# RWKV's token shift taken from TensorE's difference products to row transfers inside SBUF, mixed on VectorE before the gated unit

## The reference

```python
def rwkv7_mixer(z, mu, w0, w2, a0, a2, g2, k_k, k_a, r_k, ln_w, ln_b):
    z_prev = jnp.pad(z, ((0, 0), (1, 0), (0, 0)))[:, :-1]
    z = z + (z_prev - z) * mu.astype(f32)
    cuts = np.cumsum([D_RWKV, D_RWKV, D_RWKV, DECAY_LORA, ICL_LORA]).tolist()
    r, k, v, xw, xa, xg = jnp.split(z, cuts, axis=-1)
    w_log = -jax.nn.softplus(-(w0 + jnp.tanh(xw) @ w2)) - 0.5
    a = jax.nn.sigmoid(a0 + xa @ a2)
    g = jax.nn.sigmoid(xg) @ g2
    ...
```

## Time and profile before

| what | value |
|---|---|
| median of 3 runs | 1326.61 us (1326.31 to 1327.68) |
| profiled execution, span from first to last instruction | 1326.5 us (no other time is given for it) |
| TensorE busy | 1143.2 us, 86% |
| VectorE busy | 418.9 us, 32% |
| ScalarE busy | 208.0 us, 16% |
| GpSimd busy | 123.2 us, 9% |
| HBM read | 375.13 MB, 284 GB/s over the span |
| mean granted TensorE clock | 0.955 of full speed |

### The profile page before, as it was taken

One profiled execution on the slowest core, in us unless ns is written; L12 is line 12 of the kernel. 1 busy time (PEld: TensorE's weight loads), 2 busy tenths in 40 slices (PEclk: granted clock), 3 DMA queues, 4 the chain that ended last, 5 costly groups with the idle time before them and its releaser, 6 DMA issues.

```text
span 1326.5 us, 18979 instructions
## 1 busy us (share of the span) xinstructions
PE 1143.2 (86%) x8244; PEld 622.7 (47%) x8244; DVE 418.9 (32%) x820; ACT 208.0 (16%) x396; POOL 123.2 (9%) x148
## 2 busy tenths in 40 slices
PE   7989997986566676755899999999999799999996
PEld 6645454432222222222455467888776453333332
DVE  4255933110001000100148636641583531111113
ACT  3211431010000000000000114011240241211111
POOL 0010000100005880000025400000000000000000
PEclk9999998998889888889999999999999899999998
DMA  8422948999999999999923453111316639999991
GB/s 315 154 100 93 376 198 340 428 428 426 427 428 427 427 426 427 428 427 428 379 98 122 143 212 127 66 66 65 127 64 231 281 130 406 423 421 422 422 420 50
DMA packets 62397, 377.33 MB, mean 284 GB/s; under 512 B 6128, under 2 KB 7536, under 8 KB 37104
## 3 DMA queue, kind: packets, MB, share of 16 engines
q1 hardware_dynamic: 60736, 369.64, 68.4%
q10 hardware_dynamic: 1584, 6.55, 1.4%
HBM read 375.13 MB, written 1.05 MB: 284 GB/s over the span
## 4 chain that ended last, share of the span: by engine, by line
PE 62%; DMA 30%; DVE 4%; ACT 2%; issue 1%; SPq 0%; DVEq 0%; ACTq 0%
DMA arena<-in_w_expert_up 21%; PE psum L472 11%; PE psum L475 9%; PE psum L2749 7%; DMA arena<-in_expert_w_up 4%; PE psum L2773 3%; PE psum L1353 3%; PE psum L815 3%; DMA arena<-in_w_expert_gate 3%; PE psum L2784 3%; PE psum L2233 2%; PE psum L1383 2%; PE psum L2336 2%; PE psum L1062 2%; DMA arena<-in_w_expert_down 2%; PE psum L1969 1%
## 5 line engine op out<-in xcount | busy, mean ns | idle before, releaser
L1353 PE MATMUL psum<-arena 128*32 128x256 f32 x2048 | 147.0, 436 | 97.5 <-DMA arena<-in_w_expert_up 58.8
L472 PE MATMUL psum<-arena 128*128 128x512 f32 x352 | 157.6, 598 | 3.2 <-ACT arena L509 1.6
L1353 PEld LDWEIGHTS psum<-arena 128*32 128x32 f32 x2048 | 69.9, 121 | 175.8 <-DMA arena<-in_w_expert_up 74.6
L1383 PE MATMUL psum<-arena 128*32 128x512 f32 x512 | 124.2, 635 | 18.0 <-DMA arena<-in_w_expert_down 12.7
L475 PE MATMUL psum<-arena 128*128 128x256 f32 x544 | 122.9, 382 | 1.0 <-ACT arena L1790 1.0
L2749 PE MATMUL psum<-arena 128*64 128x512 f32 x512 | 116.0, 595 | 2.4 <-DMA arena<-in_expert_w_up 2.2
L475 PEld LDWEIGHTS psum<-arena 128*128 128x128 f32 x544 | 101.5, 189 | 16.9 <-issue 2.2
L472 PEld LDWEIGHTS psum<-arena 128*128 128x128 f32 x352 | 64.8, 190 | 81.4 <-issue 81.1
L1383 PEld LDWEIGHTS psum<-arena 128*32 128x32 f32 x512 | 31.3, 115 | 98.5 <-issue 69.3
L1414 DVE TENSOR_TENSOR arena<-arena,psum 128x256 f32<-128x256 f32 x16 | 6.8, 422 | 221.9 <-ACT arena L1397 221.9
L2749 PEld LDWEIGHTS psum<-arena 128*64 128x64 f32 x512 | 36.2, 137 | 68.8 <-issue 67.6
(11 more groups left out here) (478 smaller groups left out, 1249.1 us busy)
## 6 DMA issues: line engine op xcount, KB each, us to landing
arena<-in_w_expert_gate SPq DMA_DIRECT2D x32, 2048.0 KB, 25.2
arena<-in_w_expert_up SPq DMA_DIRECT2D x32, 2048.0 KB, 26.5
arena<-in_w_expert_down SPq DMA_DIRECT2D x31, 2048.0 KB, 25.0
arena<-in_w_in SPq DMA_DIRECT2D x21, 2048.0 KB, 8.9
arena<-in_expert_w_gate SPq DMA_DIRECT2D x32, 1024.0 KB, 11.5
arena<-in_expert_w_up SPq DMA_DIRECT2D x32, 1024.0 KB, 13.6
arena<-in_expert_w_down SPq DMA_DIRECT2D x32, 1024.0 KB, 10.2
arena<-in_w_out SPq DMA_DIRECT2D x4, 2048.0 KB, 7.8
```

The source lines that it names most:

```text
L472: mm = pe.matmul(o, lhs[:, k, sub * P:(sub + 1) * P], w[:, k, :], start=(k == 0), stop=(k == kt - 1))
L1353: mm = pe.matmul(ps[32 * c:32 * c + 32], xin[:, e, k], w[:, j, 256 * n:256 * n + 256], start=(k == 0), stop=(k == KD - 1))
L1383: mm = pe.matmul(y_ps[at:at + 32, 512 * n:512 * n + 512], hid_T4[:, j, half], w[:, j, 512 * n:512 * n + 512], start=(half == 0 and j == 0) ...
```

## The change

Two transfers from SBUF to SBUF, issued by ScalarE right after the last copy of `proj_rkv`, write the row of the token before into a new buffer `rw_before`: partitions 1 to 127 get both tiles of partitions 0 to 126 in one transfer, and partition 0's second tile gets partition 127's first tile in another. Partition 0's first tile is set to zero. VectorE then does the whole shift (`shift`) between the scan and its part of the GLU projection. TensorE's nine difference products, and its waits on `rw_moved` between the LoRA products, are gone. `rw_before` lies over the columns of gates 4 to 15, so the copy that fills gate 4 waits for the shift. ScalarE's program also does the LoRA activations, and issues the transfer of `gn`, before the fourth copy of `proj_qkv2`.

```diff
@@ ssm, vector
                 dve.memset(lora_z[:, :, 0:1], 0.0)
+                dve.memset(rw_before[0:1, 0], 0.0).then_inc(inc("rw_first_row"), 1)
@@
+        rw_before = half_ring[:, 7168:10240].rearrange("p (t c) -> p t c", t=NT)
@@ copy_or_gate
+            if out == 4:
+                act.wait_ge(*count("rw_moved", 3))
@@ rwkv
+            def move_rows(act):
+
+                for sem, n in proj_rkv.done:
+                    act.wait_ge(*count(sem, n))
+                act.dma_start(rw_before[1:P], rkv[0:P - 1]).then_inc(inc("rw_rows_moved"), 16)
+                act.dma_start(rw_before[0:1, 1], rkv[P - 1:P, 0]).then_inc(inc("rw_rows_moved"), 16)
@@ rwkv, tensor
-                for n in range(3):
-                    c = slice(512 * n, 512 * n + 512)
-                    pe.matmul(bank(2 * n), const("less_self"), rkv[:, 0, c], start=True, stop=True)
-                    pe.matmul(bank(2 * n + 1), const("less_self"), rkv[:, 1, c], start=True, stop=False)
-                    pe.matmul(bank(2 * n + 1), const("from_last"), rkv[:, 0, c], start=False, stop=True)\
-                      .then_inc(inc("rw_differences"), 1)
                 pe.wait_ge(*count("rw_lora_act", 1))
                 pe.wait_ge(*count("rw_lora_loaded", 32))
                 for n, (lhs, rhs) in enumerate(((lz[0:64, 0], wa[0:64]), (lz[64:128, 0], wa[64:128]), (lz[:, 1], wg))):
-                    pe.wait_ge(*count("rw_moved", n + 1))
@@ rwkv
-            def gpsimd(pool):
-                pass
+            def shift(dve):
...
+                for sem, n in proj_rkv.done:
+                    dve.wait_ge(*count(sem, n))
+                dve.wait_ge(*count("ssm_gelu", 1))
+                step(TT(lz, lora_z[:, :, 0:SEQ], lora_z[:, :, 1:SEQ + 1], sub))
...
+                last.then_inc(inc("rw_lora"), 1)
+                dve.wait_ge(*count("rw_first_row", 1))
+                dve.wait_ge(*count("rw_rows_moved", 32))
+                parts = [slice(512 * n, 512 * n + 512) for n in range(3)]
+                for c in parts:
+                    last = TT(rw_before[:, :, c], rw_before[:, :, c], rkv[:, :, c], sub)
+                step(last)
+                dve.wait_ge(*count("rw_rows_loaded", 16))
+                for c in parts:
+                    last = TT(rw_before[:, :, c], rw_before[:, :, c], two(mu[:, c]), mul)
+                step(last)
+                for c in parts:
+                    TT(rkv[:, :, c], rkv[:, :, c], rw_before[:, :, c], add).then_inc(inc("rw_moved"), 1)
@@ block.vector
             ssm_scan.vector(dve)
+            rwkv7.parts[1](dve)
             glu_proj.vector(dve)
@@ block.scalar
             proj_rkv.vector(act)
+            rwkv7.parts[3](act)
...
             next(rwkv_steps)
+            next(rwkv_steps)
             next(copies_beside)
```

More of the change, by code:

```diff
@@ L1807, in rwkv @@
             gg, aa, kk = tok("g"), tok("a"), tok("kk")
-            prev = take("prev", 3072, True).rearrange("p (t c) -> p t c", t=NT)
+            take("glu", 3072, True)
             first_rows, more_rows = take("first_rows", 5 * HW, True), take("more_rows", 3 * HW, True)
@@ L1814, in rwkv @@
             lz = take("lz", 2 * SEQ, True).rearrange("p (e s) -> p e s", e=2)
-            cols.release("rw_prev")
+            cols.release("rw_glu")
             ld, e1 = tok("ld", True), tok("e1", True)
@@ L2051, in tensor @@
                     mm.then_inc(inc("rw_y_turned"), 1)
-            def gpsimd(pool):
-                pass
+            def shift(dve):
+                step = vchain(dve)
+                TT, mul, add, sub = dve.tensor_tensor, ALU.mult, ALU.add, ALU.subtract
+                two = lambda a: along(a, NT, 1)
+                for sem, n in proj_rkv.done:
+                    dve.wait_ge(*count(sem, n))
+                dve.wait_ge(*count("ssm_gelu", 1))
+                step(TT(lz, lora_z[:, :, 0:SEQ], lora_z[:, :, 1:SEQ + 1], sub))
+                for e in range(2):
+                    last = dve.scalar_tensor_tensor(lz[:, e], lz[:, e], vec["mu_lora"][:, e:e + 1], lora_z[:, e, 1:SEQ + 1], mul, add)
+                last.then_inc(inc("rw_lora"), 1)
[11 more added lines that the diff above has]
+                    TT(rkv[:, :, c], rkv[:, :, c], rw_before[:, :, c], add).then_inc(inc("rw_moved"), 1)
             def vector(dve):
@@ L2059, in vector @@
                 two = lambda a: along(a, NT, 1)
+                dve.wait_ge(*count("rw_moved", 3))
                 dve.wait_ge(*count("const_again", 16))
                 dve.wait_ge(*count("glu_out", 1))
[L2062 to L2075, removed]
                 dve.wait_ge(*count("rw_lora_out", 3))
@@ L2201, in rwkv @@
             cols.release(*[n for n in list(cols.held) if n.startswith("rw_")])
-            return Stage(vector=vector, parts=(tensor, None, scalar), y=arT)
+            return Stage(vector=vector, parts=(tensor, shift, scalar, move_rows), y=arT)
         yaT = cols.take("yaT", 1024).rearrange("p (c s) -> p c s", c=4)
@@ L2999, in _ @@
             glu.scalar(act)
-            take_turns(act, "grr" + "gr" + "rr" + "gggg" + "rg" + "rrg" * 2 + "rgr" * 4 + "g" + "r" + "gg" + "tr",
+            take_turns(act, "gr" + "gr" + "rr" + "gggg" + "rg" + "rrg" * 2 + "rgr" * 4 + "g" + "r" + "gg" + "tr",
                        g=lambda act: one_more(copies_beside, copies_tail), r=lambda act: rwkv_steps, t=attention2.parts[2])
```

## The result

The changed kernel takes 1368.97 us (median of 5 runs, 1366.53 to 1370.91) against 1326.61 (5 runs): ratio 1.0314, 95% interval 1.0302 to 1.0325. It is slower, by 42.4 us; 1352.0 was forecast, with a range from 1338 to 1378. The profiled execution took 1368.97 us with a span of 1367.1, 40.6 above the span of before.

The account below looks back on a forecast made before the run. TensorE was taken as the bound. With 7.7 us saved but late rows and unit, LoRA products start at 815.9 in place of 792.54, +23.4; lower clock adds 2: 1326.6 + 25.4 = 1352.0 us, range 1338 to 1378.

Parts of the forecast that it names:

- TensorE is the bound, and the differences are worth 7.7 us: Attention tail to LoRA products: TensorE busy without a gap, so removing nine difference products takes 7.7 us off the chain.
- VectorE's 10.5 us are hidden under the GLU projection: VectorE after the LoRA shift: nine added operations take 10.5 us, covered by TensorE's 14 us of GLU projection.
- One engine carries 127 rows, at 0.459 us each: Large row transfer: 127 is prime, so one transfer engine carries all, 58.3 us in all, to 789.6 if undisturbed.
- A shift of this stage moves the end by as much: Behind the LoRA products: no transfer starts by its own clock, so the kernel's end moves by the same amount.
- ScalarE then issues 127 rows: ScalarE's queue after the last `proj_rkv` copy at 730.3: issues 1.56 MB of rows, needed at 764.4, 34 us later.
- The alternation: Shared engine: queues alternate by packet, 0.536 us a pair, so the attention's last unit takes 34.3 us, to 785.2.
- The clock: TensorE after idling 8.6 us before the LoRA products: 4 us of work at half rate lose 2 us.
- The last wait: Before the LoRA products: TensorE, done by 807.3, waits for VectorE's GLU copies to about 815.8, starting at 815.9.
- Rival 1: Row transfer: many engines carry the rows, landed by 740, gain 7.7 us, 1318.9 us; chance 12%.
- two engines would be enough: Within the many-engines rival: two engines would suffice for the rows to land by about 772.9, the deciding time.
- Rival 2: Shared engine: queues share by bytes, not packets; TensorE doesn't stall, rows take to 809.2, 1358 us; chance 18%.
- the rate of the 10 KB rows: Upper bound of the moved rows' price: 0.66 us for 12 KB, copies to 842, 1378 us; slower case 8%.

## Why the prediction was right, and where its size was off

- **TensorE is the bound, and the differences are worth 7.7 us.** Right. In the three kernels whose rows use many engines the LoRA products start 7.7 us earlier against the start of the stage (783.45, 784.53 and 785.17, with ScalarE's last copy of `proj_rkv` at 728.28, 729.37 and 730.01; before 792.54 with 729.65). At the end 5.4 to 6.8 us of them are measured: the longer issue piece in the inversion (2.76 to 3.10 us in these three, 0.77 before) takes some 2 back.
- **VectorE's 10.5 us are hidden under the GLU projection.** Right where the rows are there in time, shown by the run with 112 and 15 rows.
- **One engine carries 127 rows, at 0.459 us each.** Right: 44 of them from 741 to 761 us, below, 0.455 us each. This step decided the sign.
- **A shift of this stage moves the end by as much.** Right within 1.8 us.
- **"ScalarE then issues 127 rows"** was the step that failed. I priced the transfer and gave its issue, and the small one's behind it, nothing. The second issue stood 31.88 us, until 57 of the 127 rows had gone. That made the copy for TensorE late (16.25 us and 2.65 of clock) and, since SP's loads follow TensorE, put the unit's issue from about 747 to 764.40. Exchanging the two lines gave 9 us back.
- **The alternation.** Right in kind and in its rate, but not in how long it took. The queues of the changed kernel from 741 to 761 us, rows alone; from 793 to 805, rows beside the unit and nothing else:

```profile
q10 hardware_dynamic: 44, 0.54, 6.3%
...
q10 hardware_dynamic: 22, 0.27, 5.3%
q1 hardware_dynamic: 22, 0.05, 1.0%
```

Twenty-two for twenty-two: one packet of each in turn, 0.545 us a pair where I had 0.536. But where much else moved on the other engines a pair took longer. From 765 to 773 us, with the unit's other shares, and from 780 to 790, with ScalarE's vectors (there queue 10's packets are mostly those, and the unit's tell the pace):

```profile
q10 hardware_dynamic: 11, 0.14, 6.1%
...
q1 hardware_dynamic: 12, 0.02, 0.8%
```

Eleven rows in 8 us and twelve pairs in 10 are 0.73 and 0.83 us each. These two stretches make up some 5 of the 8 us by which the unit's 43.65 us exceed my 34.3 and 1. Also, hardly any row moved until the GLU's unit was nearly through (5 by 737, after an issue at 728.4), where I had them start after one microsecond and alternate. That cost less, since the rows then ran alone earlier: with the exchanged issues 25 of them were gone when the attention's unit was issued, where I had about 28. With the exchanged issues, which is the case that I computed, the whole makes 1359.9 in place of 1352.
- **The clock.** I had one idle time and 2 us for it; there were two, with 2.65 and 2.1.
- **The last wait.** I had VectorE's late copies as what ends last. In the changed kernel the rows landed at 805.8 and VectorE was free for its GLU copies at 816.4, 0.8 us ahead of the first one's products; the late unit alone set the time. With the issues exchanged it was VectorE, as forecast.
- **Rival 1** (many engines) had the right price, 1318.9 against 1320.4, and the wrong condition. Its aside that two engines would be enough was wrong by 27 us: the rows landed at 779 and not by 772.9, and the unit came later still. **Rival 2** (shared by bytes) is refuted by the small packets: the same bytes gave 16.0 and 44.2 us. The forecast of +25.4 against +42.4 measured lies within the range only because that reached up to another cause, the rate of the 10 KB rows, which played no part.

A version that beats both kernels is the change with its rows cut as 112 and 15 (or 126 and 1), or issued by GpSimd: 1320.4 to 1320.8 us. The three can't be told from one another by these runs.

## What to carry to other kernels

A shift by one partition is the natural way to end up with 127 rows, and 127 is prime: look at the row count of every transfer that is not a full tile, and cut it into counts with a large divisor of at most 16, as 112 and 15 or 126 and 1 here. The transfer that sat on one engine hurt twice without anyone waiting for its data: the next issue on the same queue stopped the issuing engine's whole program, and the load that passed over that engine paid one of the long packets for each of its own. In a profile it shows as an all-engine share near 1/16 with an issue of tens of microseconds beside it.

## What the runs showed of the hardware that I had not expected

- The issue of 127 rows for one engine took 1.22 us. The next one in the queue stood: it returned with 70 rows left in the changed kernel, with 71 in the run with exchanged issues (88 packets by 764.42, 32 of them not rows), and with about 100 of 762 packets of 2 KB. What the limit counts stays open.
- Rows inside SBUF moved at the rate of ordinary loads on one engine, 12 KB in 0.455 us, 27.0 GB/s, where nothing else moved.
- Beside a load issued just before it, a transfer inside SBUF began late: with the 112 rows the first packets came between 733 and 734 us, 4 to 5 after the issue at 728.9. From GpSimd, issued 4.5 us after the load that it met, 36 packets had moved by 757, 3.9 us after the issue, and the full set landed in 10.5 us. Which of the differences counts, the load's age or the queue, is open.
